# A hybrid mLSTM / RG-LRU / ConvFFN block: the first projection group fed one k-tile at a time

## What is computed

```python
n1 = rmsnorm(x, norm_mix_g[l])
proj = n1 @ w_in[l]
```

## Time and profile before

| | |
|---|---|
| time before | 1137.47 us, median of 3 runs (1136.65 to 1137.60) |
| profiled execution | span 1135.8 us from the first to the last instruction; its own device time is not given, so the 1.7 us up to the median stand for what lies around a span |
| granted TensorE clock, mean | 0.999 |
| PE busy | 1125.2 us, 99% of the span |
| DVE, ACT, POOL busy | 749.2, 578.7, 51.6 us |
| bytes moved | 213.56 MB, 188 GB/s over the span |

### The profile page before, as it was taken

The page is one execution under the profiler, slowest core; times in us unless marked ns, Lnnn a source line. Parts: engine busy times, 40 slices in busy tenths (PEclk is TensorE's granted clock), DMA queues, the critical chain, the costliest instruction groups (busy, mean ns, idle before and its releaser), DMA issues.

```text
span 1135.8 us, 18132 instructions
## 1 busy us (share of the span) xinstructions
PE 1125.2 (99%) x6030; PEld 968.0 (85%) x6030; DVE 749.2 (66%) x989; ACT 578.7 (51%) x768; POOL 51.6 (5%) x48
## 2 busy tenths in 40 slices
PE   9999999999999999999999999999999999999997
PEld 8888888888888888888888888888888888888886
DVE  6768576595776686666666666766666655556554
ACT  6656464564665664344434444443544545555454
POOL 0100100100000000000000000000000000002000
PEclk9999999999999999999999999999999999999999
DMA  8756657657555466656665665666566565655653
GB/s 265 226 161 186 191 150 205 167 166 194 183 199 196 153 185 206 190 161 215 191 184 173 211 190 165 204 201 186 167 208 195 190 196 190 194 192 186 196 190 114
DMA packets 166617, 213.56 MB, mean 188 GB/s; under 512 B 6940, under 2 KB 149532, under 8 KB 166464
## 3 DMA queue, kind: packets, MB, share of 16 engines
q1 hardware_dynamic: 165456, 210.40, 60.2%
q0 software_dynamic: 560, 2.24, 0.6%
q10 hardware_dynamic: 576, 0.60, 0.2%
HBM read 211.10 MB, written 2.11 MB: 188 GB/s over the span
## 4 chain that ended last, share of the span: by engine, by line
PE 95%; DVE 3%; ACT 1%; issue 0%; DVEq 0%; ACTq 0%
PE ps L1066 41%; PE ps L1190 27%; PE ps L1068 20%; PE ps L1062 3%; PE ps L1064 1%; DVE w L612 1%; PE ps L1161 0%; PE ps L1041 0%; DVE aT L618 0%; ACT w L351 0%; PE ps L1084 0%; PE ps L1113 0%; PE ps L1143 0%; PE ps L1133 0%; DVE xT L663 0%
## 5 line engine op out<-in xcount | busy, mean ns | idle before, releaser
L1066 PE MATMUL ps<-xT,w 128*128 128x512 f32 x2048 | 716.7, 396 | 1.0 <-DVE w L678 0.5
L612 DVE TENSOR_TENSOR w<-raw,w 128x1024 fp32r<-128x1024 f32 x391 | 479.1, 1237 | 342.9 <-ACT w L351 341.9
L351 ACT ACTIVATE w<-raw 128x1024 fp32r<-128x1024 f32 (+1 forms) x393 | 409.7, 1055 | 417.2 <-PE ps L1068 247.6
L1068 PE MATMUL ps<-xT,w 128*128 128x256 f32 x2048 | 569.2, 278 | 0.0
L1066 PEld LDWEIGHTS ps<-xT,w 128*128 128x128 f32 x2048 | 384.2, 188 | 91.1 <-DVE w L612 1.0
L1068 PEld LDWEIGHTS ps<-xT,w 128*128 128x128 f32 x2048 | 385.2, 188 | 0.2
L1190 PE MATMUL ps<-w,aT 128*128 128x512 f32 x1440 | 327.9, 389 | 0.9 <-DVE aT L618 0.9
L1190 PEld LDWEIGHTS ps<-w,aT 128*128 128x128 f32 x1440 | 269.8, 188 | 57.6 <-DVE aT L618 1.7
L351 ACT ACTIVATE fs<-fc 128x512 f32<-128x512 f32 x22 | 13.9, 632 | 101.0 <-DVE fc L962 101.0
L1025 POOL TENSOR_TENSOR fs<-fs,rB 128x512 f32<-128x512 f32 x22 | 28.4, 1293 | 569.5 <-ACT fs L351 569.5
L1062 PE MATMUL ps<-w,xT 128*128 128x512 f32 x128 | 45.2, 398 | 0.0
(11 more groups left out here) (147 smaller groups left out, 391.8 us busy)
## 6 DMA issues: line engine op xcount, KB each, us to landing
raw<-w_up_dram SPq DMA_DIRECT2D x176, 512.0 KB, 4.6
raw<-w_in_dram SPq DMA_DIRECT2D x95, 512.0 KB, 3.9
raw<-w_down_dram SPq DMA_DIRECT2D x88, 512.0 KB, 4.6
raw<-w_out_dram SPq DMA_DIRECT2D x32, 512.0 KB, 4.6
xres<-x_dram SPq DMA_DIRECT2D x3, 512.0 KB, 7.8
y_dram<-xn SPq DMA_DIRECT2D x3, 384.0 KB, 3.1
bc<-rows POOLq DMA_DIRECT2D x4, 256.0 KB, 6.9
gfin<-gfin_dram POOLq DMA_DIRECT2D x1, 1024.0 KB, 4.6
```

The source lines that it names most:

```text
L351: return sc.activation(out_, in_, fn, **kw)
L612: v.tensor_tensor(w[:, s, :, 1, :], raw[:, s, :].rearrange("p (c n) -> p c n", c=CH), w[:, s, :, 0, :], ALU.subtract).then_inc(lo_ready, 1)
L1066: mm(full, w[:, s, c, 0, cut], xT[:, kt, :, :].rearrange("p a n -> p (a n)"), start=kt == 0, stop=False)
L1068: ins = mm(rest, w[:, s, c, 1, cut], xT[:, kt, 0, :], start=False, stop=kt == KT - 1)
```

## The change

- **Loads.** SP's order becomes x 0:256, first half of unit 0, x 256:512, second half of unit 0, and for s = 1 to 3 the x block, then unit s in two halves with a semaphore each. ACT's queue issues the identity ahead of the gain. The other parameters move from ACT's queue to POOL's, and all of POOL's three loads now wait until the last x block has landed.
- **PSUM.** k-tiles 0 to 3 get a bank each (4, 5, 6, 2); the later pairs lie in banks 7, 3, 4, 5, 6, 7.
- **Order of PE.** Warm-up 6 instead of 8, keep-warm 2 instead of 6. Then P(0), b1, P(1), P(2), b2, P(3), b3; then for s = 1 to 3 the two first k-tiles of the unit, one pair of transposes, its two last k-tiles, one pair of transposes (none in s = 3).
- **ACT and DVE** follow: k-tile 0, its weights, k-tile 1, its weights, the second half of unit 0, k-tiles 2 and 3; then always two k-tiles of x and the half unit that goes with them. gw_hi stands behind all of group 0 on ACT, the five small operations, base and gw_lo behind all of it on DVE.

The lists of step names (A0, V0, E0) follow the new orders, and w_first_landed becomes one semaphore for each unit; these lines are left out here.

```diff
-WARM_UP, KEEP_WARM = 8, 6
+WARM_UP, KEEP_WARM = 6, 2
...
+        def first_place(k):
+            bank = (4, 5, 6, 2)[k] if k < CH else (7, 3, 4, 5, 6, 7)[k // 2 - 2]
+            return ps[:, bank, 0:S] if k < CH else ps[:, bank, k % 2 * S:(k % 2 + 1) * S]
+        def last_in_bank(k):
+            return k if k < CH else k | 1
...
-            def load_x(c):
-                first, last = c * BANK, (c + 1) * BANK
-                if c == 0:
-                    sp.dma_start(xres[:, :, 0:COLS], x_rows[:, :, 0:COLS]).then_inc(x_first_landed, 16)
-                    first = COLS
-                sp.dma_start(xres[:, :, first:last], x_rows[:, :, first:last]).then_inc(x_landed[c], 16)
+            def load_x(first, last, landed):
+                sp.dma_start(xres[:, :, first:last], x_rows[:, :, first:last]).then_inc(landed, 16)
+            def load_first(s, c, landed):
+                sp.dma_start(raw[:, s, c * COLS:c * COLS + BANK].rearrange("p (c n) -> p c n", c=CH // 2),
+                             in_v[s, :, c:c + CH // 2, COL_Q:COL_Q + COLS]).then_inc(landed, 16)
...
-            load_x(0)
-            sp.wait_ge(lo_ready, 1)
-            for c, landed in ((0, w_first_landed), (CH // 2, raw_landed[0])):
-                sp.dma_start(raw[:, 0, c * COLS:c * COLS + BANK].rearrange("p (c n) -> p c n", c=CH // 2),
-                             in_v[0, :, c:c + CH // 2, COL_Q:COL_Q + COLS]).then_inc(landed, 16)
+            load_x(0, COLS, x_first_landed)
+            sp.wait_ge(lo_ready, RING)
+            load_first(0, 0, w_first_landed[0])
+            load_x(COLS, BANK, x_landed[0])
+            load_first(0, CH // 2, raw_landed[0])
             for s in range(1, RING):
-                load_x(s)
-                load(0, s, in_v[s, :, :, COL_Q:COL_Q + COLS], raw[:, s, :].rearrange("p (c n) -> p c n", c=CH))
+                load_x(s * BANK, (s + 1) * BANK, x_landed[s])
+                load_first(s, 0, w_first_landed[s])
+                load_first(s, CH // 2, raw_landed[s])
...
+            act_e.dma_start(ident, const_in[:, C_ID:C_ID + P]).then_inc(ident_landed, 16)
             act_e.dma_start(par[:, PAR_GMIX:PAR_GMIX + KT], par_in[:, PAR_GMIX:PAR_GMIX + KT]).then_inc(gain_landed, 16)
-            act_e.dma_start(ident, const_in[:, C_ID:C_ID + P]).then_inc(ident_landed, 16)
-            act_e.dma_start(par[:, PAR_GMIX + KT:], par_in[:, PAR_GMIX + KT:]).then_inc(par_landed, 16)
...
+            def x_hi(k):
+                after(act_e, E0, f"k{last_in_bank(k)}")
+                did(act_fn(xT[:, k, 0, :], first_place(k),
+                           scale=par[:, PAR_GMIX + k:PAR_GMIX + k + 1]), A0, f"k{k}")
+            def first_hi(s, c, n, landed, ready):
+                act_e.wait_ge(landed, 16)
+                act_e.wait_ge(unit_used, s + 1)
+                act_fn(w[:, s, c:c + n, 0, :], raw[:, s, c * COLS:(c + n) * COLS].rearrange("p (c n) -> p c n", c=n)).then_inc(ready, 1)
             act_e.wait_ge(gain_landed, 16)
-            transposed_hi(A0, E0, PAR_GMIX, 0)
-            act_e.wait_ge(w_first_landed, 16)
-            act_e.wait_ge(unit_used, 1)
-            act_fn(w[:, 0, 0:CH // 2, 0, :], raw[:, 0, 0:BANK].rearrange("p (c n) -> p c n", c=CH // 2)).then_inc(first_hi_ready, 1)
-            transposed_hi(A0, E0, PAR_GMIX, 1)
-            act_e.wait_ge(raw_landed[0], 16)
-            act_fn(w[:, 0, CH // 2:, 0, :], raw[:, 0, BANK:].rearrange("p (c n) -> p c n", c=CH // 2)).then_inc(hi_ready, 1)
-            for r in range(ROWS):
-                squares(A0, r, 0)
-            transposed_hi(A0, E0, PAR_GMIX, 2)
-            round_units(0, [1])
-            for b in (3, 4, 5):
-                transposed_hi(A0, E0, PAR_GMIX, b)
-            round_units(0, [2])
+            for c in range(CH // 2):
+                x_hi(c)
+                first_hi(0, c, 1, w_first_landed[0], first_hi_ready)
+            first_hi(0, CH // 2, CH // 2, raw_landed[0], hi_ready)
+            for c in range(CH // 2, CH):
+                x_hi(c)
+            squares(A0, 0, 0)
+            for s in range(1, RING):
+                for c, landed, ready in ((0, w_first_landed[s], first_hi_ready), (CH // 2, raw_landed[s], hi_ready)):
+                    for k in range(s * CH + c, s * CH + c + CH // 2):
+                        x_hi(k)
+                    first_hi(s, c, CH // 2, landed, ready)
+                if s == 1:
+                    squares(A0, 1, 0)
             act_e.wait_ge(gate_landed, 16)
             after(act_e, V0, "gw_zero")
             did(act_fn(gws[:, :, 0:2, 0:H], gw[:]), A0, "gw_hi")
-            round_units(0, [3])
-            for b in (6, 7):
-                transposed_hi(A0, E0, PAR_GMIX, b)
             squares(A0, 0, 1)
             round_units(1, [0])
             for n in (1, 2):
             did(v.memset(small[:, C_EPS:C_EPS + 1], EPS), V0, "start")
...
-            transposed_lo(A0, V0, PAR_GMIX, 0)
-            dve.wait_ge(first_hi_ready, 1)
-            v.tensor_tensor(w[:, 0, 0:CH // 2, 1, :], raw[:, 0, 0:BANK].rearrange("p (c n) -> p c n", c=CH // 2),
-                            w[:, 0, 0:CH // 2, 0, :], ALU.subtract).then_inc(first_lo_ready, 1)
-            transposed_lo(A0, V0, PAR_GMIX, 1)
+            def x_lo(k):
+                after(dve, A0, f"k{last_in_bank(k)}")
+                did(v.scalar_tensor_tensor(out=xT[:, k, 1, :], in0=first_place(k),
+                                           scalar=par[:, PAR_GMIX + k:PAR_GMIX + k + 1], in1=xT[:, k, 0, :],
+                                           op0=ALU.mult, op1=ALU.subtract), V0, f"k{k}")
+            def first_lo(s, c, n, ready):
+                v.tensor_tensor(w[:, s, c:c + n, 1, :], raw[:, s, c * COLS:(c + n) * COLS].rearrange("p (c n) -> p c n", c=n),
+                                w[:, s, c:c + n, 0, :], ALU.subtract).then_inc(ready, 1)
+            for c in range(CH // 2):
+                x_lo(c)
+                dve.wait_ge(first_hi_ready, c + 1)
+                first_lo(0, c, 1, first_lo_ready)
             dve.wait_ge(hi_ready, 1)
-            v.tensor_tensor(w[:, 0, CH // 2:, 1, :], raw[:, 0, BANK:].rearrange("p (c n) -> p c n", c=CH // 2),
-                            w[:, 0, CH // 2:, 0, :], ALU.subtract).then_inc(lo_ready, 1)
-            transposed_lo(A0, V0, PAR_GMIX, 2)
-            split_units(0, [1])
-            transposed_lo(A0, V0, PAR_GMIX, 3)
+            first_lo(0, CH // 2, CH // 2, lo_ready)
+            for c in range(CH // 2, CH):
+                x_lo(c)
+            for s in range(1, RING):
+                for k in range(s * CH, s * CH + CH // 2):
+                    x_lo(k)
+                dve.wait_ge(first_hi_ready, s + CH // 2)
+                first_lo(s, 0, CH // 2, first_lo_ready)
+                for k in range(s * CH + CH // 2, (s + 1) * CH):
+                    x_lo(k)
+                dve.wait_ge(hi_ready, s + 1)
+                first_lo(s, CH // 2, CH // 2, lo_ready)
...
-            for b in (4, 5):
-                transposed_lo(A0, V0, PAR_GMIX, b)
-            split_units(0, [2])
+            norm_base(A0, V0)
             after(dve, A0, "gw_hi")
             did(v.tensor_tensor(gws[:, :, 2:4, 0:H], gw[:], gws[:, :, 0:2, 0:H], ALU.subtract), V0, "gw_lo")
-            split_units(0, [3])
-            for b in (6, 7):
-                transposed_lo(A0, V0, PAR_GMIX, b)
-            norm_base(A0, V0)
             split_units(1, [0])
...
         @block.gpsimd
         def _(pool):
+            pool.wait_ge(x_landed[RING - 1], 16)
             pool.dma_start(gw[:], gate_w).then_inc(gate_landed, 16)
+            pool.dma_start(par[:, PAR_GMIX + KT:], par_in[:, PAR_GMIX + KT:]).then_inc(par_landed, 16)
             pool.dma_start(tri, const_in[:, C_TRI:C_TRI + P]).then_inc(tri_landed, 16)
...
                 for c in tiles_of_k:
                     kt = s * CH + c
-                    if tiles and c % 2 == 0:
+                    if tiles is V0:
+                        after(pe, tiles, f"k{kt}")
+                    elif tiles and c % 2 == 0:
                         after(pe, tiles, f"t{kt // 2}")
...
-            def transpose_x(c):
-                for b in (2 * c, 2 * c + 1):
-                    pe.wait_ge(x_landed[c] if b else x_first_landed, 16)
-                    if b >= 4:
-                        after(pe, V0, f"t{b - 4}")
-                    did(transpose_bank(b), E0, f"t{b}")
+            def transpose_x(b):
+                pe.wait_ge(x_landed[b // 2] if b else x_first_landed, 16)
+                if b >= 4:
+                    after(pe, V0, f"k{(0, 1, 2, 5)[b - 4]}")
+                for kt in (2 * b, 2 * b + 1):
+                    for r in range(ROWS):
+                        ins = nc.tensor.transpose(first_place(kt)[:, r * P:(r + 1) * P], xres[:, r, kt * P:(kt + 1) * P], ident)
+                    did(ins, E0, f"k{kt}")
             transpose_x(0)
             for n in range(KEEP_WARM):
```

(29 more changed lines are left out.)

## The result

Seven executions of each kernel: 1140.44 us in the median after (1138.93 to 1141.04), 1137.29 before (1136.65 to 1138.46); the ratio is 1.0026, with a 95% interval of 1.0015 to 1.0036. The change makes the kernel about 3 us slower. The change itself is 3.15 us, where 1.1 to 1.2 was forecast.

A forecast was written before the change was run, and what follows sets the result against it. PE's work plus its idle time bounds the kernel: 2.33 us won at the start, 3.5 given back in group 0, mostly waits, gates at 24.92, +1.17 us in sum; 1138.6 us against the median, range 1136.2 to 1140.6.

The forecast's parts named there:

- chain of x: Group 0: 3.06 us from a pair's first transpose to its product, against 1.9 us of PE work, so PE waits.
- P(n) + 4.55: Group 0: earliest start of product pair P(n+2) after P(n), in us, where the work alone is 3.8.
- Part 1: The start: transposes at about 4.15 us, first product P(0) at 6.33, 2.33 us ahead of the old 8.66.
- Part 2: Stretch to k-tile 4: P(2) waits for x of k-tile 2 and starts at 8.59; bank b2 starts at 9.30.
- rival A: P(0) to P(2) and bank b1: clock rises late, products at half rate, +2.3 us, 1140.9; chance 0.12.
- half of each us past 6.5: Rival on a late clock rise: below about 9 us, it costs half of each us past 6.5.
- The gap is small beside the work before it: PE idle from about 6.0 to 6.3 us: claimed the clock still changes at the same time as before.
- 3 us fewer of dummy work: PE's start: the argument for the late clock rise, from the dummy matmuls taken away.
- B: Group 0: latency shorter than read, PE stays fed, -1.5 to -2.5 us, 1135.0 to 1136.0; chance 0.08.
- If group 0 ended over 0.9 us sooner than I say, this would be late next: Behind group 0: diag, ending at 27.7 us while the gates hold PE until 28.6, is covered by 0.9.
- Rival C: The start: weights land as late as before, about 7 us, P(0) at 8.3, +3, 1140.5; chance 0.05.

The follow-up runs named there:

- restored depth: Changed kernel with every pair of transposes from the third on one product pair earlier in PE's order: 1136.89 us; with 7 warm-up and 4 keep-warm matmuls, 1136.73 us.
- 6 and 2: Warm-up and keep-warm counts of the changed kernel; with transposes one product pair earlier 1136.89 us; the kernel before with only these counts set, 1137.44 us.
- 7 and 4: 7 warm-up and 4 keep-warm matmuls instead of 6 and 2: changed kernel with transposes one product pair earlier 1136.73 us, changed kernel with only these counts 1140.26 us.
- PE's waits filled: Changed kernel with 4, 2 and 2 matmuls of ones put into PE's waits ahead of k-tiles 4, 8 and 12: 1140.36 us.
- the repeat: The changed kernel once more, nothing edited, for more executions and a second profile: 1140.21 us, ratio 1.0021.
- small loads early: Changed kernel without POOL's wait for the last x block, so its three loads are issued at once: 1140.39 us, ratio 1.0026.
- 6 and 6: Changed kernel with 6 keep-warm matmuls instead of 2, warm-up left at 6: 1139.82 us, ratio 1.0020.
- k-tile 2 ahead: Changed kernel with earlier transposes, 7 warm-up, 4 keep-warm, and k-tile 2 of x before unit 0's second half of weights on ACT and DVE: 1136.49 and 1136.46 us.
- x in halves: Changed kernel with transposes one product pair earlier, 7 warm-up and 4 keep-warm matmuls, and x blocks 1 to 3 loaded in halves of 256 columns: 1137.39 us.

## Why the prediction was right, and where it wasn't

**The chain of x: right, to a few hundredths.** The step that decides was the 3.06 us from the first transpose of a pair to the product that uses it, of which PE's work covers 1.9. Measured from the profile above: 9.88 to 12.92, 3.04 us. "P(n) + 4.55": 12.92, 17.47 and 22.03 are 4.55 and 4.56 apart. The waits are at k-tiles 4, 8, 12 and 14 and the releaser is the split, as forecast. The restored depth takes 3.3 us away (6 and 2) and 3.5 (7 and 4), more than the 2.6 us of waits behind k-tile 3, since b2 then no longer hangs on P(2).

**The start: right in direction, 0.4 us too good.** Part 1 has the transposes at 4.15. They started at 4.51, for x 0:256 landed at 4.35 instead of the 4.1 that I carried over from the old trace; ACT took k-tile 0 at 5.28 instead of 4.88, and P(0) was at 6.77 instead of 6.33. The first weights landed at 5.25 instead of 5.0, but nothing waited for them. This is the term of the sum that was mis-sized: from P(0) to P(2) it is 2.33 us where I had 2.26 (and 2.33 and 2.34 in the profiles with PE's waits filled and with 6 keep-warm matmuls), so 0.44 of the 0.51 us by which P(2) was late (9.10, not 8.59) were there at P(0). Runs that undo the load order or the small loads' delay don't show this in the median, within noise of about its size.

**The term that was left out** is in Part 2: "P(2) needs x of k-tile 2 ... ACT 7.54". ACT takes the second half of the weights first, and I took these as landed without a line of their own. In the run where they landed at 8.8, P(2) came 1.90 us after ACT took them up (8.80 to 10.70). From the 7.18 of the first profile that gives 9.08, an estimate, against the 9.10 that P(0) gives: a tie there. In the seven profiles of the changed order of PE it decides alone only once, at 8.8; in the five others ACT waits for PE's transposes, so P(0) and the clock decide.

From P(2) on everything is a fixed sum, 16.28 us where I had 16.33, so the gates were at 25.38, not 24.92. Against the profiled execution the error looks smaller than it is: span 1137.0 forecast, 1137.1 measured, since the stretch behind the gates came out 0.35 us shorter than before, for a reason that no run shows. That these two errors cancel is luck.

**The clock.** I gave rival A 0.12, with its price of 2.3 us. Of the six profiles with the changed order of PE and 2 or 4 keep-warm matmuls, three had products at the lower level (the repeat, the one with the small loads early and the one with the old load order), with gates at 26.8 to 27.1. So the chance was far too small, and the price too high: by my rule, half of each us past 6.5, a rise at 10.9 costs 2.2 us, and the repeat shows 1.45. "The gap is small beside the work before it" was argued from one old profile, in which PE was busy without a pause up to 8.2 us; "3 us fewer of dummy work" is 1.9 by the prices that I read (two at 0.44 and four at 0.25). The Trainium skill (TensorE: Matmul & The Clock Gate, Part 1) calls the throttled clock the default. The traces agree: PE starts at 1.2 GHz in every one. Its warm-up takes 2.90 us for 12 records and 3.33 for 14, 0.22 a record, where keep-warm matmuls with the clock up take 0.61 for 4 and 1.06 for 8, 0.11 a record.

The number 1138.6 was thus the time of a good execution given as that of the median: over the 18 executions of the changed kernel the times are 1138.93 to 1141.32, their median 1140.4, and the best four lie at 1138.9 to 1139.5. With the fixed stretch behind the gates, the median execution has them at about 26.8, an estimate (1140.4 less the 1.8 around a span and 1111.8). How much of the 1.5 us between is the clock and how much the landing isn't settled: each was seen in a profile to cost 1.4 to 1.6 us, but only profiled executions show it, and more dummies brought nine of eleven times together (6 and 6) or did nothing (7 and 4).

**The range.** The median lay 0.16 us inside its upper end, and three of the seven executions above it, so that it held is in part luck; the two sources of the extra 1.5 us were priced outside it or not at all. It doesn't take in "B's near end" either: B was 1135.0 to 1136.0, below 1136.2.

**The rest.** gw_lo had a cover of 0.64 us (24.74 against 25.38; forecast 0.6), diag one of 0.64 (28.41 against 29.05; forecast 0.9), and no wait shows that the late loads of POOL cost the changed kernel anything; the halving of the units was never undone by itself. "If group 0 ended over 0.9 us sooner than I say, this would be late next" was too strict: with the gates at 22.5 to 22.9 diag was still in time, for the squares came sooner with them. At 22.1 it was late by 0.2 us, behind POOL's gw. With x in halves it was the parameters, at 22.7, which I had put at 22 at the latest. Rival B fell for the changed kernel; with the depth restored the gates came at 22.7 and 22.9, not at its 21.3, with 1.3 us of waits for x still on the wire. Rival C's premise (weights at about 7) was never seen.

## What to carry over

When an order is written by hand for the first tiles, count for each wait how much work of the bound engine lies between the instruction that starts a chain and the one that uses it; feeding in smaller pieces shortens the first latency once, but cuts this cover every time (here from a unit or more to a pair and a bank, 1.9 us for a chain of 3.04). A head start is worth only what the last of the inputs lets through: find what the *second* step waits for, the load, the entry ahead of it in the queue, and the first step itself, and write down a time for each. A start that depends on the clock and on single landings has to be forecast for the middle of many executions, not for the one in the profile.

## What the runs showed of the hardware

- PE began at the 1.2 GHz level in every profile; it went to 2.4 GHz somewhere between 4.4 and 10.9 us. In the two profiles of the changed kernel PE's work is the same up to the first product (6.77 and 6.69), and in one this product runs at 2.4 GHz, in the other all up to 10.9 us at 1.2.
- A granted clock of 1.00 in the rows ahead of the first change says nothing: in the slow start of the repeat it reads 1.00 with products at half the rate, and 0.50 appears only after a rise and a fall (8.6 to 12 us in the kernel before with 6 and 2). Both falls seen came within 0.6 us of the first product's start, behind an idle PE of 1.39 us there and 1.23 with the small loads early; an idle PE of 1.62 us ahead of k-tile 2 (7 and 4) brought none.
- The fourth 256 KB load of one queue, issued at 2.3 us in each of the eleven profiled executions with these first four loads, landed between 6.8 and 8.8 us. The three ahead of it kept within 0.6 us in eight of the ten whose small loads came late. In the others the third landed at 6.95 instead of 5.7 to 6.2 (k-tile 2 ahead, the second time), and the first at 5.0 instead of 4.1 to 4.4 (x in halves).
